# The second attention's side work: the convolution inputs' products in one portion at each step instead of two

## The reference, cut to what matters

```
z = h @ w_in
c_q, c_kv, k_r, u_glu, gate_logits = split(z)
q = rms_norm(c_q) @ w_uq            # 8 heads of 128 + 64 (rotated) columns
k_nope, v = rms_norm(c_kv) @ w_uk, rms_norm(c_kv) @ w_uv
s = (q_nope @ k_nope.T + q_rope @ k_rope.T) * scale, causal
attn = softmax(s) @ v               # in blocks of 128 queries
a, b = split(u_glu)                 # 1024 channels each
u = a * sigmoid(b)                  # the convolution's input
u = silu(layer_norm(conv31(u) + conv_b))
```

## Time and profile before

| | us |
|---|---|
| median of 3 runs | 3069.12 |
| lowest and highest | 3068.59, 3072.71 |
| the profiled execution's own time | 3073.17 |
| its span | 3071.2 |
| TensorE busy | 2717.3 (88%) |
| VectorE busy | 1569.0 (51%) |
| ScalarE busy | 1043.9 (34%) |
| granted TensorE clock, mean over the span | 0.929 |

### The profile page before, as it was taken

One profiled execution on the slowest core, in us unless ns is written; L12 is line 12 of the kernel. 1 busy time (PEld: TensorE's weight loads), 2 busy tenths in 40 slices (PEclk: granted clock), 3 DMA queues, 4 the chain that ended last, 5 costly groups with the idle time before them and its releaser, 6 DMA issues.

```text
span 3071.2 us, 29431 instructions
## 1 busy us (share of the span) xinstructions
PE 2717.3 (88%) x11760; PEld 1952.1 (64%) x11760; DVE 1569.0 (51%) x2840; ACT 1043.9 (34%) x1737; POOL 15.8 (1%) x20
## 2 busy tenths in 40 slices
PE   6988888888999588987996899977989999999997
PEld 2566666653334355555774788854767877778776
DVE  4224563544756556679635544465653323343534
ACT  1034545331111322323423333323574334442222
POOL 0000000000000000000000000000000000000000
PEclk9987888988999798888998999988999999999999
DMA  6111000238995310020231222212212242313221
GB/s 172 41 42 30 28 14 1 82 143 357 374 381 230 124 43 21 21 76 20 97 110 55 77 88 110 83 43 69 83 55 83 83 108 57 96 59 106 82 71 40
DMA packets 178749, 295.99 MB, mean 96 GB/s; under 512 B 26160, under 2 KB 120752, under 8 KB 170416
## 3 DMA queue, kind: packets, MB, share of 16 engines
q1 hardware_dynamic: 175088, 282.52, 26.3%
q0 software_dynamic: 2304, 8.39, 0.7%
q10 hardware_dynamic: 1216, 3.15, 0.3%
HBM read 288.79 MB, written 4.19 MB: 95 GB/s over the span
## 4 chain that ended last, share of the span: by engine, by line
PE 53%; DVE 10%; ACT 3%; issue 1%; DVEq 0%; ACTq 0%
PE ps L316 14%; PE ps L317 14%; PE ps L318 14%; PE ps L324 7%; DVE arena L1856 3%; PE ps L1927 2%; DVE t L369 1%; DVE t L353 1%; PE ps L339 1%; DVE t L2178 0%; PE ps L1949 0%; PE ps L2010 0%; ACT L2587 0%; DVE arena L2160 0%; DVE ws0l L302 0%
## 5 line engine op out<-in xcount | busy, mean ns | idle before, releaser
L302 DVE TENSOR_TENSOR ws0l<-w,ws0h 128x1024 fp32r<-128x1024 f32 (+2 forms) x125 | 135.5, 1084 | 149.9 <-ACT ws0h L294 149.8
L302 DVE TENSOR_TENSOR ws1l<-w,ws1h 128x1024 fp32r<-128x1024 f32 (+1 forms) x124 | 137.8, 1111 | 139.6 <-ACT ws1h L294 139.4
L1856 DVE SCALAR_TENSOR_TENSOR arena<-arena 128x512 f32<-128x512 f32 x240 | 180.3, 751 | 7.4
L324 PE MATMUL ps<-arena 128*128 128x512 f32 (+11 forms) x440 | 149.3, 530 | 27.2 <-DVE arena L1976 22.8
L294 ACT ACTIVATE ws0h<-w 128x1024 fp32r<-128x1024 f32 (+2 forms) x125 | 117.7, 942 | 134.2 <-PE ps L318 130.4
L294 ACT ACTIVATE ws1h<-w 128x1024 fp32r<-128x1024 f32 (+1 forms) x124 | 119.5, 963 | 116.2 <-PE ps L318 108.3
L302 DVE TENSOR_TENSOR ws2l<-w,ws2h 128x1024 fp32r<-128x1024 f32 (+1 forms) x94 | 102.1, 1086 | 89.5 <-ACT ws2h L294 89.5
L1527 PE MATMUL ps<-w,arena 128*64 128x512 f32 x512 | 129.2, 642 | 19.6 <-issue 18.2
L324 PE MATMUL ps<-t,con 128*128 128x512 f32 (+1 forms) x68 | 46.0, 771 | 105.6 <-DVE t L353 86.1
L316 PE MATMUL ps<-hpc_hi,ws0h 128*128 128x512 f32 x320 | 128.0, 400 | 6.2 <-DVE ws0l L302 4.1
L316 PE MATMUL ps<-hpc_hi,ws1h 128*128 128x512 f32 x328 | 130.9, 399 | 1.5 <-issue 1.5
(11 more groups left out here) (531 smaller groups left out, 6232.4 us busy)
## 6 DMA issues: line engine op xcount, KB each, us to landing
w<-in_w_gate_up SPq DMA_DIRECT2D x32, 2048.0 KB, 15.6
w<-in_w_in SPq DMA_DIRECT2D x37, 1024.0 KB, 5.4
w<-in_w_down SPq DMA_DIRECT2D x32, 1024.0 KB, 11.3
w<-in_w_ff SPq DMA_DIRECT2D x16, 2048.0 KB, 8.1
w<-in_w_in SPq DMA_DIRECT2D x13, 2048.0 KB, 8.3
w<-in_w_in SPq DMA_DIRECT2D x48, 512.0 KB, 5.2
w<-in_w_branch SPq DMA_DIRECT2D x6, 2048.0 KB, 7.8
w<-in_w_out SPq DMA_DIRECT2D x4, 2048.0 KB, 8.0
```

Of the source, the lines that this page charges most:

```text
L302: e.go.tensor_tensor(p[1], tiles[t][1], p[0].bitcast(F32), ALU.subtract).then_inc(*e.inc(lo, ("lo", t)))
L324: i = e.go.matmul(bank, lt, rt, start=j == 0, stop=j == n - 1)
L1856: i = e.go.scalar_tensor_tensor(out=cv[:, m, :], in0=ureg[:, m % 2, k:k + 512], scalar=cw[:, m, k:k + 1], in1=cv[:, m, :], op0=ALU.mult, o ...
```

## The change: all of a step's fills behind its scores

The second call of `fill_pe` in a step goes, and the first takes all of the step's fill matmuls:

```diff
             for t in range(STEPS2):
-                middle = (dealt(t - 1) + dealt(t) + 1) // 2
                 if t < NU2:
...
                     products(e, ps[t % 2][:, 0:n], [(qn[:, P * i:P * i + P], kn[:, 0:n]), (qr[0:64, P * i:P * i + P], kr[0:64, 0:n])],
                              ("s2", t))
-                fill_pe(e, middle)
+                fill_pe(e, dealt(t))
                 if 0 <= t - 2 < NU2:
...
                     products(e, ps[4][:, P * i:P * i + P], [(vv[:, P * j:P * j + P], p[:, P * j:P * j + P]) for j in range(i + 1)],
                              ("o2", t - 3))
-                fill_pe(e, dealt(t))
                 if t < NU2:
                     hh, i = units2[t]
                     if i in (2, 1) and hh < 7:
                         head2_pe(e, hh + 1, 2 - i)
```

## The result

The kernel with one portion is slower. Five timed runs on one chip gave a median of 3083.14 us (3081.27 to 3089.74), five of the kernel before beside them 3070.25 us (3068.59 to 3072.71): a ratio of 1.0047 [1.0032, 1.0061], +12.9 us by the medians and +14.4 by the ratio. Run again later, it gave 3080.67 us, +9.2 by the medians, and a ratio of 1.0037 [1.0025, 1.0050], which is +11.4. The intervals share 1.0032 to 1.0050, which is +9.8 to +15.4 us. The forecast was +8.0 and 3077.1 us.

What follows compares the result with a forecast made beforehand. It took the stage as a relay, TensorE up to block 0's scores, then VectorE. Waits of 4.65 + 1.39 + 0.93 = 6.97 us and 1 for the clock gave +8.0 on 3069.12, so 3077.1 us, range 3070.5 to 3084.5.

Steps and rivals of the forecast that it cites:

- What bounds it: Each head's round: TensorE from first scores to those of block 0, then VectorE to the next head.
- First and second terms: TensorE waits for q's copy behind the later o2: 4.65 us over steps 6, 10, 14, 22, 26; 1.39 in step 18.
- Third, step 7: In step 7 t2 comes four fills later, moving ScalarE's copy, sigmoid and split and VectorE's rotation by 0.93 us.
- Fourth, the seams: Behind o2's narrow products, scores or a projection follow instead of a fill: taken as nothing, between -1.8 and +1.8 us.
- the taps' tail keeps its length: At the stage's end, VectorE's closing run of taps was to last as long as before.
- Sixth, the clock, +1: Six new TensorE waits bring two half-clock stretches, part of them in slack: +1 us.
- one in three: Of the stage's waits of about this length looked at, one in three cost half of some 3.4 us, 1.7 us.
- +12.2: Upper end of the forecast itself: seams at +1.8 us and two clock stretches of 1.7 us in full.
- No change: The 22.8 us of idle ahead of the heads' first scores swallow the shift: 3069 to 3070 us; chance 0.20.
- Slower still: Each new wait is followed by half a clock on part 1: +17.2 us, 3086.3 us; chance 0.12.
- Faster: New waits draw slow stretches into block 0's slack, 3.2 us a head; with all six 12.2 faster, 3056.9 us; chance 0.06.

Runs made afterwards that it cites:

- The third buffer: A third buffer for q, added to the changed kernel (3073.68 us, ratio 1.0013) and to the kernel before (3067.77 us, ratio 0.9989).
- e1: Changed kernel, but with two portions again in the steps of block 1: 3073.84 us, ratio to the kernel before 1.0009.
- e2: Kernel before, with one portion in the steps of block 1 alone: 3073.61 us, ratio 1.0008.
- the filled pair: Kernel before and changed kernel, each with dummy matmuls in TensorE's idle ahead of the heads: 3056.80 us (0.9943) and 3061.90 us (0.9971).
- e4: Kernel before, with all of a step's fills in one portion behind o2: 3072.93 us, ratio 1.0003.
- e6: Kernel before, with a third q buffer: 3067.77 us, ratio 0.9989.
- e3: Kernel before with dummy matmuls in TensorE's idle ahead of the heads, and only step 7 in one portion: one profiled execution, stage 272.49 us.
- e5: Changed kernel, with a third q buffer: 3073.68 us, ratio to the kernel before 1.0013.
- e7: Kernel before, with dummy matmuls in TensorE's idle ahead of the heads: 3056.80 us, ratio 0.9943.
- e8: Changed kernel, with dummy matmuls in TensorE's idle ahead of the heads: 3061.90 us, ratio to the kernel before 0.9971.
- e9: Kernel before, with both a third q buffer and dummy matmuls in the idle ahead of the heads: 3053.96 us, ratio 0.9942.

## Why the prediction was right and wrong

*What bounds it: right.* TensorE up to the scores of block 0 and then VectorE; every wait put on the path lengthened it, and the slack ahead of the heads stayed.

*First and second terms, o2 and the copy of q: right, in place and size.* 5.96 us for 6.04. The third buffer takes out these waits, all but head 4's for k, and e1 and e2 show them apart. *Third, step 7: right,* 0.91 for 0.93, once more alone with 0.90. *Fourth, the seams: right at nothing.* In the filled pair the third, fourth and sixth rounds differ by 0.91, 0.92 and 0.94, which is the four moved fills and no more.

*The step that failed* is the sentence in the third term that called the even tiles' ends in steps 13, 24 and 30 "nothing". It asked only whether VectorE waits for the weight split. It left out the bank: the sigmoid also frees the one bank that all fills share, and TensorE stands there. This costs 0.4 us in step 25 and, together with step 31's own single portion, 0.9 in the tail. With them "the taps' tail keeps its length" was wrong too. For step 13 "nothing" held. The second failure is that the sum ends with the stage: the 2.1 us behind it were put at nothing without a reason. So the sum of 6.97 us of waits and 1 of clock was too small, 8.0 for a measured +12.9 in the first series: the runs show 8.2 of waits and 2.1 behind the stage, and the rest stays open.

*Sixth, the clock, +1: mis-sized, and wrong in sign within the stage.* The six waits of 0.75 us brought no slow stretches of their own. Its "one in three" came from one execution: in the other two of the kernel before, the same wait of 1.08 us is followed by no fall of the clock for 8.3 us, and the wait grown to 1.46 by none for 40.8 and 9.8 us in the changed kernel. The granted clock in the stage went from 0.88 and 0.89 to 0.89 and 0.90, in e2, with all six, to 0.92. One slow stretch did come with the change, in a place that the term didn't name: behind the wait of 2.37 us in step 31. The Trainium skill's rule, "TensorE: Matmul & The Clock Gate", "A second HAM failure mode: psum-queue depth-cycling", by which small idles would make the clock swing, is not borne out by waits of this length. What does bring slow stretches here is the idle of 2.3 us and more ahead of the heads: filled, it gives 15 us back. Behind the stage the sign is the other one. Before, then changed, from the eighth L1087, which ends the merge, to the ninth:

```profile
1521.83:2414.33 892.50, 792.45 (x3441) 635.14 (x3442) 457.57 (x709) 357.06 (x522) 0.00 (x0) 0.94 0.22 76
```

```profile
1528.10:2422.87 894.77, 795.03 (x3441) 636.97 (x3442) 457.24 (x710) 357.04 (x522) 0.00 (x0) 0.94 0.22 76
```

Here 2.3 us go, with the same instructions. The merge is not the place: its first sum comes 0.81 us later behind L316 (13.64 for 12.83), but its eighth 0.43 earlier (115.38 for 115.81), and from the ninth to the end it is 656.96 for 656.85. Added up over the record of the granted clock, the stretch shown has 109.2 us at 1.2 GHz in the changed kernel and 102.4 in the one before. In all executions the merge starts inside a slow stretch. Where this one ends 3.0 to 3.5 us behind L316 (before three times, e1, e2, e4, e6), the part behind the stage has 132.3 to 132.6 us at 1.2 GHz and takes 1664.9 to 1665.2; where it ends 4.8 to 5.9 us behind (changed twice, e3, e5, e7, e8, e9), it has 133.8 to 138.6 and takes 1666.4 to 1667.8. Since e7 and e9, whose steps are those of before, are among the latter, it goes with where the slow stretches happen to fall; what sets that is not shown.

*The sum.* 8.2 of waits and 2.1 behind make 10.3 us, inside both measured intervals (9.8 to 18.7 and 7.7 to 15.4); the forecast's 8.0 is inside the second alone. The second series lies around the sum (+9.2 by the medians, +11.4 by the ratio). In the first, 2.6 us to the medians and 4.1 to the ratio are left, and that is not settled. The timed executions of the kernel before scatter from 3061 to 3080 us, those of the changed one from 3076.8 to 3089.7. Of the 4.7 us between the means of the changed kernel's two series, some 2.8 are clock by the line above, an estimate (0.9292 against 0.9307). But the same line leaves the change at 10.5 to 12.4 us with the clock taken out, 2 to 4 more than its waits, and both profiled executions show the stage below the sum of its waits, so an unlucky clock is not shown to be the whole of it.

*The baseline, and luck.* Against profiled executions the forecast was nearly met: 3081.2 forecast, 3081.82 and 3081.28 measured. That is partly luck. The waits it had left out (1.3 us) and the loss behind the stage (2.1) were made up by a stage with less time at 1.2 GHz (62.6 and 56.2 us against 65.0 to 67.7) and by the 1.1 us less ahead of it. The 4.05 us by which the profiled execution of before lay above the median did not carry over: the changed kernel's profiled executions lie 1.3 us below and 0.6 above their medians. As an absolute time the forecast was 3077.1 and is 6.0 us under 3083.14; 1.1 of this is that five runs of before have a median of 3070.25 and the three that were shown 3069.12. The range's upper edge, 3084.5, follows from no term of the sum: its own +12.2 gives 3081.3.

*The rivals.* No change: excluded. Slower still: its mechanism, half a clock on part 1, did not appear, though the time came half way to it. Faster: the slow stretches were worth more than the change costs, as that rival said (its 3.2 us a head; e7 shows 15 us in all), but a wait of 0.75 us in part 1 does not draw them off.

## What to carry to other kernels

When work that a consumer stood behind is moved ahead of a producer, follow the shifted copy to everything that it releases, banks as well as data. Read the cost between two events of an engine that repeat to hundredths, and not from rounds in which the clock changes: one half of this change had 6 us of waits and measured as nothing. In this stage, a relay with idles of 2 us on TensorE, filling them was worth more (0.6%) than any order of the work that was tried.

## What the runs showed of the hardware

By the record of the granted clock none of the six waits of 0.75 us was followed by a fall to 1.2 GHz within 11 us, in neither execution of the changed kernel nor in e2. The idles of 2.3 us and more ahead of the heads were followed by one, or already inside a slow stretch when they ended, in most rounds. The wait of 2.37 us in step 31 was too, in all five executions that have it (changed twice, e2, e5, e8): the clock is at half for 3.4 us, from between 0.3 us ahead of the wait's end and 0.9 behind it. The wait of 1.45 us at the same place in the others was followed by no fall within 11 us. Nine matmuls in such an idle (19 and 20 in the two long ones), whose result nobody reads, kept most heads at 2.4 GHz: the stage's mean went from 0.88 to 0.96, its time at 1.2 GHz from 67.7 to 21.8 us.

The Trainium skill, "ScalarE: Activation LUTs", "What ACT_TABLE_LOAD costs", states about 1283 ns for the load and 1380 ns for a drain with it. This case shows the load, 1.28 us, and no drain beside it: in step 25 the load starts at 1344.35 and the sigmoid at 1345.64, 0.01 us behind its end.
